# Stick-breaking attention: in each step VectorE's quarter sums and low parts first, scan and product last

## The chip, the cores and the metric

The kernel runs on one core of one Trainium2 chip. The metric is the device time of one execution in microseconds (us), taken as the median of several runs.

## The reference, cut to what matters

Two transformer blocks run one after the other on a sequence of 1024 rows of width 1024, in float32. The first has pooling, a sliding-window attention, a feed-forward part and a gate; the second has two kinds of attention, an output projection and a gated feed-forward part with a short convolution. The change lies in the second block's stick-breaking attention (8 heads of 64 features):

```python
for blk in range(s // SB_BLOCK):                 # 8 blocks of 128 queries
    logits = einsum("bqhd,bkhd->bhqk", q[:, q_start:k_end], k[:, :k_end]) * scale
    strict = (q_start + arange(SB_BLOCK))[:, None] > arange(k_end)[None, :]
    log_beta = log_sigmoid(logits)
    log_keep = where(strict, log_sigmoid(-logits), 0.0)
    log_tail = cumsum(log_keep, reverse=True) - log_keep
    weights = where(strict, exp(log_beta + log_tail), 0.0)
    outs.append(einsum("bhqk,bkhd->bqhd", weights, v[:, :k_end]))
```

The weight of a key is sigmoid(logit) times the product of sigmoid(-logit) over all later keys that the query may see. The kernel makes this product with a running multiplication, a scan, instead of logarithms.

## The kernel before, in words

Float32 products are made in three passes of a faster format: each operand is split in a high part (rounded by ScalarE, `..._hi`) and a low part (source minus high part, made by VectorE, `..._lo`). Every result that becomes an operand again so passes ScalarE first and then VectorE.

The stage around the change handles 4 pairs of heads. For each pair, `BSTEPS` lists 24 blocks: for each query tile `qt` of 128 rows, for each of the two heads, a first chunk of up to four key tiles and, for `qt` above 3, a second chunk with the rest. A block has 1 to 4 tiles of 128 keys. All 96 blocks (`NS`) are numbered by z; `stick_step(z)` gives pair, head, query tile, chunk and tiles. Each engine runs a loop over steps s written out by hand, in which it handles different blocks, so that the stages of one block follow each other:

- ScalarE, step s: `turned_hi(s-3)` (L2049) rounds the turned weights from PSUM to `wt` (L2054), then `signs(s)` (L2038) makes `keep` = sigmoid(-x) (L2044) and `stick` = sigmoid(x) (L2047) from the logits; then high parts of projections and weights, and for a finished quarter `quarter_low` (L2060) and `quarter_move` (L2065). `signs(s)` waits for VectorE's product of block s-2.
- GpSimd, step s: `cut(s)` (L864) zeroes `stick` on and above the diagonal for blocks with a diagonal; then the sums of finished quarters (L875) and of their squares (L884, L890, L893).
- VectorE, step s: `tails(s-1)` (L2669) makes the scan over `keep` into `tail` (L2675) and the product `stick` times `tail` (L2682), which waits for `stick` or the cut; `turned_lo3(s-3)` (L2684) makes the low half of the turned weights in `wt` from PSUM (L2687), and waits for ScalarE's rounded half of block s-3, made in the same step s; `quarter_add(d)` (L2690) adds the two halves of a quarter of the output (L2692) five steps after the quarter's last block, 32 times in all. Behind these stand `job_lo` (low parts of the projection for the next pair, L2301, L2305, L2308), `beside3` (in step 16 the inverse roots for another normalisation, L2698 to L2704; near the end the output weights L2718 and the turned rows L2712) and `stick_weight_lo` (low part of a weight unit, L2288).
- TensorE, step s: `turn3(s-2)` (L1547) transposes the weights of block s-2; it waits for VectorE's product of s-2 and for the low part of s-4. `outputs3(s-4)` (L1563) multiplies turned weights and values. In odd steps `scores3(s+1)` (L1513) makes the logits of the next two blocks and waits for `stick` of block s. Then `jobs3` (L918 to L920) makes a part of the next pair's projection (steps 0 to 71), and in steps 78 to 93 `first_half_row` makes the first half of the output projection.

The order in each engine's loop is the only thing that sets the order of its work. VectorE's loop is L2740 to L2756:

```python
for s in range(NS + 7):
    if 1 <= s <= NS:
        tails(s - 1)
    if 3 <= s < NS + 3:
        turned_lo3(s - 3)
    d = quarter_ended(s - 5)
    if d is not None:
        quarter_add(d)
```

Of the kernel before, what the change touches and what calls it, by code (L numbers as in the profile page):

```python
# [72 lines left out]
class Chain:  # L73
# [13 lines left out]
    def link(self, ins):  # L87
        ins.then_inc(self.sem, 1)
        self.n += 1
        if self.at is None:  # L90
            self.eng.wait_ge(self.sem, self.base + self.n)
        else:
            self.eng.wait_ge(self.sem, self.at * self.per + (self.base + self.n))


def build(nc, x, p, w_in, w_pool, pool_scale, attn_sinks, w_out, ln1_g, ln1_b, w_ff1, w_ff2,
# [8 lines left out]
    with ctx:  # L105
# [318 lines left out]
        NS = 4 * NB  # L424

        def stick_step(z):

            hh, qt, c = BSTEPS[z % NB]
            nt = qt - 3 if c else min(qt + 1, 4)
            return z // NB, hh, qt, c, nt, 0 if c else qt + 1 - nt  # L430
# [6 lines left out]
        def diagonals(z):  # L437

            return sum(stick_step(i)[3] == 0 for i in range(z + 1))
# [13 lines left out]
        def quarter_ended(z):  # L453

            return quarter_of(z) if 0 <= z < NS and stick_step(z)[2:4] in ((1, 0), (3, 0), (5, 1), (7, 1)) else None
# [7 lines left out]
        def quarter_bank(hh):  # L463

            return pt[:, hh, :].rearrange("p (a b n) -> p a b n", b=2, n=P)
# [39 lines left out]
        def stick_ends(s):  # L505

            return [job[:4] for job in stick_jobs(s) if job[4] == KT - 1]
# [81 lines left out]
        def next_unit(q, e):  # L589

            u = {1: 3 * q + 2, 3: 3 * q + 3, 6: 3 * q + 4}[e]
            return u if u < 24 else None
# [9 lines left out]
        def _(sp):  # L602
# [19 lines left out]
            for c, (u, slot, _, _) in enumerate(SEG["in"]["rows"]):  # L622
                room("in", None, c)
                if c < 2:
                    for r in range(4 * c, 4 * c + 4):
                        sp.dma_start(acc[:, r, :], x[r * P:(r + 1) * P, :]).then_inc(x_in[c], 16)
                if c < 6:
                    col = c * P if c < 4 else 1024 + (c - 4) * P
                    sp.dma_start(raw_k(slot, 0, 8), w_in_t[:, :, col:col + P]).then_inc(raw_in[slot], 16)
                else:  # L630
                    for hh in range(2):
                        col = 512 + 64 * (c - 6) + 256 * hh
                        sp.dma_start(raw_k(slot, 0, 8)[:, :, 64 * hh:64 * hh + 64],
                                     w_in_t[:, :, col:col + 64]).then_inc(raw_in[slot], 16)
# [60 lines left out]
            with sp.Fori(0, SEG["gate"]["n"]) as i:  # L695
                for c, (u, slot, _, _) in enumerate(SEG["gate"]["rows"]):
                    room("gate", i, c)
                    sp.dma_start(raw_k(slot, 0, 8), gate_t[:, :, ds((i * 2 + c) * P, P)]).then_inc(raw_in[slot], 16)
                    sp.dma_start(raw_k(slot, 8, 10), ple_t[:, :, ds((i * 2 + c) * P, P)]).then_inc(raw_in[slot], 16)
# [1512 lines left out]
        def _(dve):  # L2212
# [71 lines left out]
            def stick_weight_lo(u):  # L2284
                if u is not None:
                    hi, lo, src, _, n = stick_unit(u)
                    dve.wait_ge(split_hi, n)
                    dve.tensor_tensor(lo, src, hi.bitcast(F32), ALU.subtract).then_inc(w_ready, 1)  # L2288

            def job_lo(i, n, kv, ends, q, q_slot=0, one=False):  # L2290

                for e, kind, half in ends:
                    if kind == "V":
                        continue
                    dve.wait_ge(jb_hi, i * (2 * NJ2) + (n + e + 1))
                    bank = 0 if one else BANK3[e] if q is not None and q != "alone" and q >= 5 else half
                    src = pd[:, q_slot if kind == "Q" else 0, bank * HB:(bank + 1) * HB]
                    cols = slice(half * HB, (half + 1) * HB)
                    if kind == "Q":
                        hi, lo = kv["q"]  # L2300
                        dve.scalar_tensor_tensor(out=lo[:, cols], in0=src, scalar=QSCALE, in1=hi[:, cols].bitcast(F32),  # L2301
                                                 op0=ALU.mult, op1=ALU.subtract).then_inc(jb_lo, 1)
                    elif kind == "K":
                        hi, lo = kv["k"]
                        dve.tensor_tensor(lo[:, cols], src, hi[:, cols].bitcast(F32), ALU.subtract).then_inc(jb_lo, 1)  # L2305
                    else:
                        v = kv["v"][:, 4 * half:4 * half + 4, :, :]
                        dve.tensor_tensor(v[:, :, :, 64:P], src.rearrange("p (r h c) -> p r h c", h=2, c=64),  # L2308
                                          v[:, :, :, 0:64].bitcast(F32), ALU.subtract).then_inc(jb_lo, 1)
# [359 lines left out]
            def tails(z):  # L2669
                pair, hh, qt, c, nt, kt0 = stick_step(z)  # L2670
                f, n, c1 = hh, nt * P, S - (qt + 1 - kt0 - nt) * P
                kept = keep[:, z % 2, 0:n][:, ::-1]
                dve.wait_ge(b_keep, z + 1)
                bound = kept if c else passed[:, HB - n:HB][:, ::-1]
                link(dve.tensor_tensor_scan(tail[:, f % 2, c1 - n:c1][:, ::-1], kept, bound,  # L2675
                                            tail[:, f % 2, c1:c1 + 1], ALU.mult, ALU.min if c else ALU.max))
                w = stick[:, z % 3, 0:n]
                if c:
                    dve.wait_ge(b_stick, z + 1)
                else:  # L2680
                    dve.wait_ge(b_cut, diagonals(z))
                dve.tensor_tensor(w, w, tail[:, f % 2, c1 - n + 1:c1 + 1], ALU.mult).then_inc(b_w, 1)  # L2682

            def turned_lo3(z):  # L2684
                n = stick_step(z)[4] * P
                dve.wait_ge(b_wh, z + 1)
                dve.tensor_tensor(wt[:, z % 2, 1, 0:n], pt[:, 2 + z % 2, 0:n], wt[:, z % 2, 0, 0:n].bitcast(F32),  # L2687
                                  ALU.subtract).then_inc(b_ws, 1)

            def quarter_add(d):  # L2690
                dve.wait_ge(q_low, d + 1)
                dve.tensor_tensor(quarter[d % 2][:, :, :], quarter_bank(d % 2)[:, :, 0, :], quarter[d % 2][:, :, :],  # L2692
                                  ALU.add).then_inc(q_added, 1)
# [27 lines left out]
            def beside3(s):  # L2721
                if s == 16:
                    dve.wait_ge(oa_sq, 8)
                    inverse_roots(rsq_a[:, :], ssq[:, 0:8], HB)
                    dve.sem_inc(oa_roots, 1)
                if 72 <= s < 76:
                    mix_weight_lo(s - 72)
                if 75 <= s < 79:
                    for b in range(2 * (s - 75), 2 * (s - 74)):
                        mixed_lo(b, pd[:, 0, b % 2 * HB:(b % 2 + 1) * HB])  # L2730
                if s == 80:
                    dve.sem_inc(m_free, 8)
                if 94 <= s < 98:
                    mix_weight_lo(s - 90)
                if 95 <= s < 97:
                    for b in range(2 * s - 182, 2 * s - 180):
                        mixed_lo(b)

            link(dve.memset(tail[:, :, S:S + 1], 1.0))
            for s in range(NS + 7):  # L2740
                if 1 <= s <= NS:
                    tails(s - 1)
                if 3 <= s < NS + 3:
                    turned_lo3(s - 3)
                d = quarter_ended(s - 5)
                if d is not None:
                    quarter_add(d)
                if 1 <= s <= 3 * NB + 2:
                    for q, e, kind, half in stick_ends(s - 1) + stick_ends(s - 2):
                        if (kind == "T") == ((q, e, kind, half) in stick_ends(s - 1)):  # L2750
                            job_lo(0, 4 * NJ1 + NJ2 * q, att2[q % 2], [(e, kind, half)], q)
                beside3(s)
                if 1 <= s <= 3 * NB + 2:
                    for q, e, kind, half in stick_ends(s - 2):
                        if kind != "T" and half:
                            stick_weight_lo(next_unit(q, e))  # L2756
# [168 lines left out]
```

## Time and profile before

| | us |
|---|---|
| median of 3 runs | 2544.61 |
| lowest and highest run | 2543.91, 2546.9 |
| the profiled execution | 2542.35 |
| its span, first to last instruction | 2540.4 |
| TensorE busy in the span | 2449.6 |
| VectorE busy | 1499.6 |
| ScalarE busy | 848.3 |
| GpSimd busy | 278.6 |

The mean granted clock of TensorE is 0.990 of full speed. Busy times of TensorE count overlapping matmuls by their covered time. The stick-breaking loop runs from about 1458 to 1751 us of the span. PE is TensorE, PEld its weight load, DVE VectorE, ACT ScalarE, POOL GpSimd.

### The profile page before, as it was taken

What the parts mean: (1) busy time and instruction counts of PE and PEld (TensorE: products, weight loads), DVE (VectorE), ACT (ScalarE), POOL (GpSimd) and SP (SyncE); (2) the same over time, 40 slices, a digit from 0 to 9 for tenths busy, and PEclk for the clock granted to TensorE, in tenths of its full rate; (3) what the DMA queues carried; (4) which work ended last, traced back from release to release, by engine and by line L of the source; (5) the groups of instructions that cost most, each with busy time, mean ns of one, the idle gap of its engine ahead of it and who ended that gap; (6) DMA issues with size and microseconds to landing.
All of it is one profiled execution on the core that took longest, in us unless ns stands there. A gap on an engine that the chain in (4) does not pass through costs nothing.

```text
span 2540.4 us, 31692 instructions
## 1 busy us (share of the span) xinstructions
PE 2449.6 (96%) x11970; PEld 2027.8 (80%) x11970; DVE 1499.6 (59%) x2087; ACT 848.3 (33%) x1517; POOL 278.6 (11%) x212
## 2 busy tenths in 40 slices
PE   8999999999999999998999999988999999999998
PEld 6787878888888888787788877767788888888886
DVE  5685564444434447546444499977675555656466
ACT  2374421011101102536444476665612020212122
POOL 4333100000000000001222233331000000000000
PEclk9999999999999999998999999998999999999999
DMA  4553032232322223113111001021111120202011
GB/s 124 32 43 121 21 100 79 75 104 82 91 88 91 87 76 113 38 38 121 34 41 31 26 18 34 17 100 42 42 60 57 34 66 22 70 23 74 25 59 75
DMA packets 201574, 156.99 MB, mean 62 GB/s; under 512 B 56185, under 2 KB 176513, under 8 KB 201473
## 3 DMA queue, kind: packets, MB, share of 16 engines
q1 hardware_dynamic: 183344, 124.94, 17.0%
q10 hardware_dynamic: 18128, 30.71, 4.8%
q8 instruction: 63, 1.03, 0.2%
q14 instruction: 39, 0.31, 0.0%
HBM read 147.23 MB, written 11.56 MB: 63 GB/s over the span
## 4 chain that ended last, share of the span: by engine, by line
PE 86%; DVE 7%; ACT 3%; issue 2%; DMA 1%; SPq 0%; POOL 0%; ACTq 0%; DVEq 0%; POOLq 0%
PE pd L918 25%; PE pd L920 25%; PE pd L919 25%; PE pt L1471 1%; PE pd L1513 1%; PE pd L1440 1%; DVE tail L2675 1%; PE pt L1563 1%; PE pt L1489 1%; PE pt L1547 1%; PE pt L938 1%; PE pt L918 1%; PE pt L919 1%; PE pt L920 1%; DVE wt L2687 0%
## 5 line engine op out<-in xcount | busy, mean ns | idle before, releaser
L918 PE MATMUL pd<-actT_hi,st_hi 128*128 128x512 f32 x1872 | 745.6, 398 | 7.0 <-DVE st_lo L2458 3.5
L920 PE MATMUL pd<-actT_hi,st_lo 128*128 128x512 f32 x1872 | 732.2, 391 | 0.0
L919 PE MATMUL pd<-actT_lo,st_hi 128*128 128x512 f32 x1872 | 731.5, 391 | 0.0
L918 PEld LDWEIGHTS pd<-actT_hi,st_hi 128*128 128x128 f32 x1872 | 353.0, 189 | 82.8 <-issue 8.7
L920 PEld LDWEIGHTS pd<-actT_hi,st_lo 128*128 128x128 f32 x1872 | 352.7, 188 | 75.8
L919 PEld LDWEIGHTS pd<-actT_lo,st_hi 128*128 128x128 f32 x1872 | 353.4, 189 | 66.1
L918 PE MATMUL pd<-mv_hi,hid_hi 128*128 128x512 f32 x864 | 337.0, 390 | 3.8 <-DVE acc L2763 1.5
L919 PE MATMUL pd<-mv_lo,hid_hi 128*128 128x512 f32 x864 | 336.2, 389 | 0.0
L920 PE MATMUL pd<-mv_hi,hid_lo 128*128 128x512 f32 x864 | 336.2, 389 | 0.0
L1863 ACT ACTIVATE mv_hi<-raw 128x1024 fp32r<-128x1024 f32 x54 | 55.9, 1056 | 602.3 <-PE pd L920 477.9
L1708 ACT ACTIVATE evac<-pd 128x1024 f32<-128x1024 f32 x76 | 77.9, 1024 | 451.2 <-PE pd L920 451.2
L2421 DVE TENSOR_TENSOR acc<-acc,pd 128x1024 f32<-128x1024 f32 x72 | 87.9, 1221 | 184.7 <-PE pd L920 184.7
L814 POOL TENSOR_TENSOR st_hi<-raw,ones 128x1024 fp32r<-128x1024 f32 x27 | 65.8, 2439 | 1192.7 <-DMA raw<-in_w_in 906.1
L918 PEld LDWEIGHTS pd<-mv_hi,hid_hi 128*128 128x128 f32 x864 | 162.2, 188 | 39.3 <-DVE acc L2763 2.9
L920 PEld LDWEIGHTS pd<-mv_hi,hid_lo 128*128 128x128 f32 x864 | 162.2, 188 | 33.8
L919 PEld LDWEIGHTS pd<-mv_lo,hid_hi 128*128 128x128 f32 x864 | 162.2, 188 | 33.4
L2458 DVE TENSOR_TENSOR st_lo<-raw,st_hi 128x1024 fp32r<-128x1024 f32 (+1 forms) x83 | 103.6, 1250 | 118.9 <-ACT st_hi L1863 113.4
L2762 DVE TENSOR_TENSOR gated<-pd,row_b 128x1024 f32<-128x1024 f32 x48 | 58.8, 1225 | 103.5 <-PE pd L920 103.2
L1863 ACT ACTIVATE st_hi<-raw 128x1024 fp32r<-128x1024 f32 (+1 forms) x83 | 89.0, 1075 | 55.7 <-DMA raw<-in_w_ff 20.3
L2845 DVE TENSOR_SCALAR cv<-evac,cw,cb 128x1024 f32<-128x1024 f32 x44 | 35.7, 811 | 119.3 <-ACT evac L1708 118.1
L2458 DVE TENSOR_TENSOR mv_lo<-raw,mv_hi 128x1024 fp32r<-128x1024 f32 x54 | 65.0, 1223 | 59.5 <-ACT mv_hi L1863 58.3
L2620 DVE CUSTOM_DVE_ANT_0 prob<-pd,bias 128x640 f32<-128x640 f32 (+4 forms) x64 | 42.0, 658 | 82.2 <-PE pt L1471 80.5
(354 smaller groups left out, 3577.6 us busy)
## 6 DMA issues: line engine op xcount, KB each, us to landing
raw<-in_w_ff SPq DMA_DIRECT2D x64, 512.0 KB, 4.0
ada_raw<-in_w_ada ACTq DMA_DIRECT2D x64, 384.0 KB, 3.2
raw<-in_w_up SPq DMA_DIRECT2D x44, 512.0 KB, 3.8
raw<-in_w_in SPq DMA_DIRECT2D x30, 512.0 KB, 3.8
raw<-in_w_down SPq DMA_DIRECT2D x22, 512.0 KB, 3.3
acc<-in_x SPq DMA_DIRECT2D x16, 512.0 KB, 6.6
raw<-in_w_out SPq DMA_DIRECT2D x12, 512.0 KB, 3.2
raw<-in_w_ple_gate SPq DMA_DIRECT2D x8, 512.0 KB, 3.7
```

The costliest lines, as they stand in the source:

```text
L814: pool.tensor_tensor(hi.rearrange("p (k n) -> p k n", n=P), src.rearrange("p (k n) -> p k n", n=P), ones[:, :].unsqueeze(1).to_broadcast([ ...
L918: pe.matmul(out_ap, a_hi, b_hi, start=start, stop=False, skip_group_check=check)
L919: pe.matmul(out_ap, a_hi, b_lo, start=False, stop=False, skip_group_check=check)
L920: return pe.matmul(out_ap, a_lo, b_hi, start=False, stop=stop, skip_group_check=check)
L938: last = pe.transpose(pt[:, job % 4, r * P:(r + 1) * P], src[:, half * 4 + r, kt * P:(kt + 1) * P], ident[:, :])
L1708: act.activation(buf[:, t % 2, :], pd[:, t % 2, :], func, **kw).then_inc(t_free, 1)
L1863: act.activation(hi, src, ACT.Copy).then_inc(split_hi, 1)
L2421: return dve.tensor_tensor(acc[:, r, :], acc[:, r, :], pdr(r), ALU.add)
L2458: dve.tensor_tensor(lo, src, hi.bitcast(F32), ALU.subtract).then_inc(w_ready, 1)
L2620: dve.tensor_tensor_reduce(out=prob2[:, z % 2, 0:n], in0=x, in1=bias2[pair % 2][:, hh, NA - n:NA], scale=-1.0, scalar=3e38, op0=ALU.add, o ...
L2762: link(dve.tensor_tensor(gt[:, :], pdr(r), row_gate[:, :], ALU.mult))
L2845: link(dve.tensor_scalar(y, u, cw[:, 2, ds(f, 1)], cb[:, ds(f, 1)], ALU.mult, ALU.add))
```

## The change

In VectorE's loop the three calls that open a step are put in the opposite order: the quarter sum first, then the low part of the turned weights, and scan and product last of the three. What follows them in the step keeps its place. Each call issues the same instructions with the same waits as before, and no other engine's program is touched.

```diff
             for s in range(NS + 7):
-                if 1 <= s <= NS:
-                    tails(s - 1)
-                if 3 <= s < NS + 3:
-                    turned_lo3(s - 3)
                 d = quarter_ended(s - 5)
                 if d is not None:
                     quarter_add(d)
+                if 3 <= s < NS + 3:
+                    turned_lo3(s - 3)
+                if 1 <= s <= NS:
+                    tails(s - 1)
                 if 1 <= s <= 3 * NB + 2:
                     for q, e, kind, half in stick_ends(s - 1) + stick_ends(s - 2):
```

## Rows read from the trace of the kernel before

**Rows 1.** The page: the span, and VectorE's busy time and share.
```profile
span 2540.4 us, 31692 instructions
...
PE 2449.6 (96%) x11970; PEld 2027.8 (80%) x11970; DVE 1499.6 (59%) x2087; ACT 848.3 (33%) x1517; POOL 278.6 (11%) x212
```

**Rows 2.** Stretches: length, busy us (instructions) of PE PEld DVE ACT POOL, clock, DMA.
```profile
1690.00:1737.00 47.00, 46.67 (x254) 37.37 (x252) 27.76 (x39) 26.86 (x54) 12.31 (x14) 1.00 0.00 0
...
sum 300.00, PE 276.37 PEld 220.37 DVE 260.04 ACT 199.71 POOL 100.79; mean PE 27.64 PEld 22.04 DVE 26.00 ACT 19.97 POOL 10.08
```

**Rows 3.** VectorE's groups by shape, 1457 to 1757: busy, mean ns | idle before.
```profile
L2675 DVE TENSOR_TENSOR_SCAN tail<-keep,tail,passed 128x512 f32<-128x512 f32 x40 | 55.0, 1375 | 0.5 <-ACT keep L2044 0.2
L2682 DVE TENSOR_TENSOR stick<-stick,tail 128x512 f32<-128x512 f32 x48 | 42.3, 880 | 3.9 <-POOL stick L864 2.7
L2687 DVE TENSOR_TENSOR wt<-pt,wt 128x512 fp32r<-128x512 f32 x48 | 32.9, 686 | 15.2 <-ACT wt L2054 15.0
...
L2692 DVE TENSOR_TENSOR quarter_b<-pt,quarter_b 128x256 f32<-128x256 f32 x16 | 6.6, 415 | 1.0 <-ACT quarter_b L2060 1.0
```

**Rows 4.** Waits, 1457 to 1757: who for whom, total us, times, longest.
```profile
DVE wt L2687 <- ACT wt L2054: 20.2, 20, 2.6
...
PE pt L1547 <- DVE wt L2687: 10.9, 7, 4.2
```

**Rows 5.** Timeline around block 9: start us, us, engine, line.
```profile
1479.95 0.69 DVE L2687 TENSOR_TENSOR wt<-pt,wt 128x512 fp32r<-128x512 f32 x1 [0.88 <-ACT wt L2054]
1480.56 0.68 DVE L2301 SCALAR_TENSOR_TENSOR q_lo2b<-pd,q_hi2b 128x512 fp32r<-128x512 f32 x1
1481.16 1.24 DVE L2288 TENSOR_TENSOR st_lo<-raw,st_hi 128x1024 fp32r<-128x1024 f32 x1
1481.41 1.59 POOL L875 TENSOR_TENSOR rows<-rows,quarter_b 64x256 f32<-64x256 f32 x1
1482.32 1.76 DVE L2675 TENSOR_TENSOR_SCAN tail<-keep,tail,passed 128x512 f32<-128x512 f32 x1
1482.93 0.60 PE L1547 MATMUL pt<-ident,stick 128*128 128x128 f32 x4
1484.12 0.92 DVE L2682 TENSOR_TENSOR stick<-stick,tail 128x512 f32<-128x512 f32 x1
1484.96 0.68 DVE L2687 TENSOR_TENSOR wt<-pt,wt 128x512 fp32r<-128x512 f32 x1
1485.78 0.63 PE L1547 MATMUL pt<-ident,stick 128*128 128x128 f32 x4 [0.40 <-DVE wt L2687]
```

**Rows 6.** Timeline around block 41.
```profile
1566.97 0.42 DVE L2687 TENSOR_TENSOR wt<-pt,wt 128x256 fp32r<-128x256 f32 x1
...
1569.04 1.31 DVE L2675 TENSOR_TENSOR_SCAN tail<-keep,tail,passed 128x512 f32<-128x512 f32 x1
1570.38 0.69 DVE L2682 TENSOR_TENSOR stick<-stick,tail 128x512 f32<-128x512 f32 x1
1570.99 0.42 DVE L2687 TENSOR_TENSOR wt<-pt,wt 128x256 fp32r<-128x256 f32 x1
1572.26 0.60 PE L1547 MATMUL pt<-ident,stick 128*128 128x128 f32 x4
```

**Rows 7.** Timeline around block 16, then around block 37.
```profile
1503.48 0.42 DVE L2687 TENSOR_TENSOR wt<-pt,wt 128x256 fp32r<-128x256 f32 x1
...
1504.14 0.60 PE L1547 MATMUL pt<-ident,stick 128*128 128x128 f32 x4
...
1561.05 0.28 DVE L2687 TENSOR_TENSOR wt<-pt,wt 128x128 fp32r<-128x128 f32 x1
1561.89 0.60 PE L1547 MATMUL pt<-ident,stick 128*128 128x128 f32 x4
```

**Rows 8.** Timeline around block 88, where TensorE has extra work.
```profile
1712.34 0.42 DVE L2687 TENSOR_TENSOR wt<-pt,wt 128x256 fp32r<-128x256 f32 x1 [1.33 <-ACT wt L2054]
...
1718.80 0.60 PE L1547 MATMUL pt<-ident,stick 128*128 128x128 f32 x4
```

## The prediction

> **What bounds the kernel now.** I read the page first: the span is 2540.4 us and VectorE is busy for 59% of it [rows 1]. The change touches one loop only, the stick-breaking stage, so next I cut the span into stretches. The stage fills the stretch from 1457 to 1757. There TensorE is busy for 276.4 of 300 us and VectorE for 260.0 [rows 2]. VectorE is close behind TensorE here, unlike in the rest of the kernel. So about 24 us of TensorE's idle time is at stake, and any time by which VectorE comes later than TensorE can bear.
>
> I call the 96 rounds of work blocks, 0 to 95. In its step s TensorE turns block s-2 and multiplies block s-4 with the values; VectorE makes the scan and the product of block s-1 and the low part of block s-3. The turn of block z waits for two things: the product of z and the low part of z-2. Both are made by VectorE in one step, z+1. **Which of them comes first inside the step is therefore nothing to TensorE**; it waits for the later one. The waits of the stage say so: TensorE waits 10.9 us in 7 places for a low part, the last piece of VectorE's step, and VectorE itself waits 20.2 us in 20 places for ScalarE's rounded half, which its low part needs [rows 4]. It is this second wait that the change moves.
>
> **The change part by part.** Nothing is added or removed. No DMA and no other queue is moved; each step issues the same VectorE instructions in another order.
>
> The prices: for a block of four tiles the scan averages 1.38 us, the product 0.88, the low part 0.69, and a quarter sum takes 0.42 [rows 3].
>
> 1. The low part goes ahead of scan and product. The scan and product of block s-1 need ScalarE's outputs of step s-1, the low part of s-3 needs ScalarE's rounded half of the same step s, and that needs TensorE's turn of s-3 and product of s-5. Before, VectorE had scan and product to do while that half was made; now it stands still until it lands and has scan and product behind it. In the 20 places where VectorE waited already, the start of the low part is set from outside and stays; scan and product, done before it until now, come after it. VectorE is then behind by one scan and product, 1569.04 to 1571.07, 2.03 us for four tiles [rows 6].
>
> What is late next: the product of the step, so TensorE's turn, and behind it, in VectorE's queue, the low parts of the projections and weights. Where TensorE has slack this costs nothing. In the timeline VectorE ends its step ahead of most turns, at block 37 by 0.56 (the low part ends at 1561.33, the turn starts at 1561.89) [rows 7] and at most others by more. Late in the stage the slack is largest: the low part of block 86 starts at 1712.34 after a wait and the turn of block 88 at 1718.80 [rows 8]. With 0.42 for the low part and 2.03 for scan and product, VectorE would end at 1714.8, still 4.0 us ahead. The 16 steps in which TensorE also makes the first half of the output product (about 60 us) cost nothing; if TensorE's 12 extra passes were gone there, the cover would be too.
>
> It costs where an external wait is followed by a long step. **Block 9** is the clearest [rows 5]. The low part of block 6 starts at 1479.95, after a wait of 0.88. Then come a projection's low part (1480.56), a weight's (1481.16), scan and product of block 9 (1482.32 and 1484.12, ending 1485.04) and the low part of 7, which ends at 1485.64; the turn of block 9 starts at 1485.78, 0.14 later. There is no slack. In the new order the same start gives: low part 0.61 (start to start), scan and product of block 8 2.03, the two low parts 1.76, low part of 7 0.60, scan and product of block 9 2.03 clean or 2.72 as now beside GpSimd. That ends at 1486.98 to 1487.67, against 1485.64: late by 1.34 to 2.03. I take 1.5, nearer the low end, because GpSimd's work (from 1481.41) would fall mostly beside the weight's low part and only a little beside a scan. The turn of block 8 (1482.93) is met: its product would end at 1482.6. The place recurs in each of the three pairs of heads that project the next pair (blocks 9, 33, 57): 3 x 1.5 = **4.5 us**.
>
> **Block 41** [rows 6]: here the low part of 38 starts at 1566.97. New order: 0.34, then 2.03, the two low parts 1.76, the next low part 0.34, then 2.03: ends at 1573.47, where now the step's end is 1570.99 + 0.42 = 1571.41. Late by 2.06; the turn stands at 1572.26, 0.85 later, of which 0.14 is the hand-over, so 0.71 is slack: **1.35 us**. The third pair has no weight to split at that place (the stream ends), so it has no such loss.
>
> **Blocks 16 and 17**: now the low part of 14 ends at 1503.90 and the turn of 16 starts at 1504.14 [rows 7], again no slack. The inverse roots lie before it. The full 2.03 of displaced work would show here, of which 1.5 was already paid at block 9: **0.6 us**. Two near misses, block 37 and its like in the third pair, 61, I put at 0.1 each, **0.2**.
>
> 2. The quarter sum goes to the front. It was behind scan, product and low part; now it delays the product by 0.42 in 32 of the steps [rows 3]. In none of the places above does such a step come before the late turn; elsewhere slack hides it. If the slack there were gone it would be 32 x 0.42 = 13.4 us, the upper bound. On the other side ScalarE, which moves the quarter on, gets it up to 2 us earlier. ScalarE isn't what TensorE waits for at the late turns, so I take 0.
>
> 3. The final steps (94, 95), where TensorE waits up to 4.2 us [rows 4], are set by the output weights' parts, which stand behind the moved pieces in both orders: 0.
>
> Sum: 4.5 + 1.35 + 0.6 + 0.2 = **+6.65 us**. The stage's lost time isn't won back later: what follows is serial. The profiled execution took 2542.35 us (span 2540.4 and 1.95 around it); with the sum, 2549.0. It lies 2.3 us under the median of the runs, 2544.61. The forecast is for the median: 2544.61 + 6.65 = **2551.3 us**. A measurement of this kernel can tell about 0.2%, 5.1 us, from no change.
>
> **A rule against the trace.** A product of four tiles takes 0.69 when alone, yet 0.92 where GpSimd works beside it, and a scan then 1.76 instead of 1.31 [rows 5, 6]. The low part, with one input in PSUM, keeps 0.68 to 0.69. The Trainium skill (SBUF, "Who interferes with whom") says that a VectorE instruction with two SBUF inputs contends with a GpSimd instruction that reads SBUF, one with at most one SBUF input doesn't. The trace agrees. Taken to its end, the rule would have the change gain, since the immune low part now fills the moment in which GpSimd runs: that is the second rival.
>
> **The rivals.**
> *All hidden.* Seven stalls in 96 steps is few; if ScalarE's halves come earlier, helped by the earlier quarter sums, each loss shrinks to under 0.7. For it: most turns have slack. Against it: at blocks 9, 33, 57 the slack is zero and the start is fixed by ScalarE, busy without a gap. Time: 0 to +4, so about 2546.6. Chance 0.27.
> *Faster, by the collisions.* Mechanism: GpSimd's cut releases the product and GpSimd's next sum together, so they collide. The 48 large products average 0.19 above 0.69, 9 us, and the 40 large scans about 0.07 above 1.31, 3 us [rows 3, 6]. If the new order keeps them apart and VectorE's ready halves cost no wait, the stalls on VectorE (10.9 us) fall by up to 5: 2540. It decides only if at block 9 more than the displaced 2.03 comes back; the two collisions there give 0.69. Chance 0.07.
> *Lag spreads to ScalarE.* ScalarE's step s waits for the product of s-2 before it makes the next keep and stick values, and TensorE's scores of every second step wait for these. If the later product holds this ring, each of the 36 pairs of steps before the sheltered stretch loses about 0.3: +11, and 2562 with the sum's 6.65. For it: VectorE waits for ScalarE in 20 places already. Against it: scores stand behind turn and outputs, which wait for the same product. Chance 0.13.
> *My forecast*, the named places and nearly no others, +4 to +10: chance 0.53.
>
> **How the numbers follow.** Faster by over 0.2%: 0.05 (the collision case, less its mild part). Slower by over 0.2%: 0.13 plus the part of the forecast above 5.1 us, 0.45 of its 0.53, in all 0.58. Within: 0.37. The range runs from 2544.5 (nearly all hidden) to 2559 (most of the spreading case); outside remain the gains and the worst of the spreading.
>
> **What would show it.** In the new profile the wait of the low part for ScalarE should grow from 20.2 us to 50 or more while VectorE's busy time stays within a few us of 260. TensorE's wait should change its name, from the low part to the product, and be some 7 us larger, at blocks 9, 17, 33, 41, 57. The stretch of 47 us before 1737 should keep its length. It is wrong if block 9's turn isn't later, or if the growth is spread evenly over all pairs of steps, or if VectorE's busy time falls by over 8 us.

## The result and the profile after

| | before | after |
|---|---|---|
| median, us (20 runs of each on the same chip) | 2545.54 | 2554.26 |
| lowest and highest run | 2542.40, 2550.01 | 2548.20, 2559.77 |
| the profiled execution | 2542.35 | 2555.22 |
| its span | 2540.4 | 2553.3 |
| mean granted clock | 0.990 | 0.987 |

The ratio of after to before is 1.0033 [1.0027, 1.0039]: the change costs 8.7 us. The forecast was slower, 2551.3 in a range of 2544.5 to 2559.0.

First the page of after, answering [rows 1]:

```profile
span 2553.3 us, 31692 instructions
...
PE 2458.4 (96%) x11970; PEld 2031.1 (80%) x11970; DVE 1492.7 (58%) x2087; ACT 850.6 (33%) x1517; POOL 280.7 (11%) x212
```

VectorE is busy for 6.9 us less in a span 12.9 us longer. So the change saves busy time and still loses time: what it costs must be waits. In the after trace the first turn of the stage starts at 1464.73, against 1462.55 before, with no changed instruction ahead of it. These 2.18 us are a difference between two executions and are left out from here on: every "later by" below counts from the turn of block 0 in the same trace.

Next the waits of the stage, 1457 to 1772 us of after (who waits for whom, total us, times, longest), answering [rows 4]:

```profile
DVE wt L2687 <- ACT wt L2054: 40.6, 35, 2.5
ACT keep L2044 <- DVE stick L2682: 30.4, 31, 2.4
...
PE pt L1547 <- DVE stick L2682: 17.6, 13, 4.1
```

The low part waits for ScalarE's rounded half in 35 places instead of 20 and for twice as long, 40.6 us instead of 20.2. TensorE's wait has changed its name, from the low part to the product, and grown from 10.9 to 17.6 us. A third wait has grown most: ScalarE waits 30.4 us for the product, where the same view of before has 4.9 us in 6 places.

VectorE's groups by shape over 1457 to 1770 (busy us, mean ns | idle before), answering [rows 3]:

```profile
L2675 DVE TENSOR_TENSOR_SCAN tail<-keep,tail,passed 128x512 f32<-128x512 f32 x40 | 52.7, 1317 | 0.0
L2682 DVE TENSOR_TENSOR stick<-stick,tail 128x512 f32<-128x512 f32 x48 | 36.4, 757 | 1.7
L2687 DVE TENSOR_TENSOR wt<-pt,wt 128x512 fp32r<-128x512 f32 x48 | 32.9, 686 | 13.6 <-ACT wt L2054 13.2
```

The products have become faster by 5.9 us and the scans by 2.3; the low parts took 32.9 us before and take 32.9 now. This is where VectorE's lower busy time comes from.

Then stretches of after (length; busy us and instructions of PE, PEld, DVE, ACT, POOL; granted clock; DMA share; GB/s), answering [rows 2]:

```profile
1457.00:1770.00 313.00, 284.66 (x1584) 225.16 (x1585) 252.09 (x392) 201.76 (x443) 102.64 (x124) 0.95 0.13 43
1702.00:1749.00 47.00, 47.00 (x256) 37.80 (x255) 27.00 (x40) 26.63 (x56) 11.67 (x14) 1.00 0.00 1
1558.00:1562.00 4.00, 4.00 (x15) 2.69 (x15) 2.67 (x7) 2.34 (x5) 1.01 (x2) 0.58 0.00 0
```

TensorE is again busy for all of the sheltered 47 us. The last of the three rows is new in kind: TensorE is busy for all 4 us, but at a granted clock of 0.58 (1.00 is full speed).

To find where the time goes I took the start of TensorE's turn (L1547) of each block in both traces and subtracted. The lateness grows in a few jumps:

| turn of block | later by, us | what was added since the row above |
|---|---|---|
| 8 | 0.00 | |
| 9 | 1.08 | 1.08 at block 9 |
| 32 | 1.78 | 0.38 at 13, 0.12 at 14, 0.34 at 16, 0.31 at 17 and 18, -0.50 at 20, 0.05 after |
| 33 | 3.21 | 1.43 |
| 34 | 4.72 | 1.51, at the lower clock |
| 38 | 5.56 | 0.73 at 37, 0.11 at 38 |
| 42 | 6.85 | 1.10 at 41, 0.20 at 42 |
| 56 | 6.84 | nothing |
| 57 | 8.18 | 1.34 |
| 58 | 9.70 | 1.52, at the lower clock |
| 62 | 10.54 | 0.73 at 61, 0.11 at 62 |
| 78 to 91 | 10.5 | nothing (between 71 and 77 it moves from 9.7 to 11.4 and back) |
| 95 | 10.41 | |

Block 9 shows the mechanism. The timeline of after (start us, us, engine, line, out<-in, idle before), answering [rows 5]:

```profile
1482.12 0.69 DVE L2687 TENSOR_TENSOR wt<-pt,wt 128x512 fp32r<-128x512 f32 x1 [1.83 <-ACT wt L2054]
1482.73 1.27 DVE L2675 TENSOR_TENSOR_SCAN tail<-keep,tail,passed 128x512 f32<-128x512 f32 x1
1484.04 0.69 DVE L2682 TENSOR_TENSOR stick<-stick,tail 128x512 f32<-128x512 f32 x1
1484.65 0.68 DVE L2301 SCALAR_TENSOR_TENSOR q_lo2b<-pd,q_hi2b 128x512 fp32r<-128x512 f32 x1
1485.25 1.21 DVE L2288 TENSOR_TENSOR st_lo<-raw,st_hi 128x1024 fp32r<-128x1024 f32 x1
1486.38 0.68 DVE L2687 TENSOR_TENSOR wt<-pt,wt 128x512 fp32r<-128x512 f32 x1
1486.99 1.27 DVE L2675 TENSOR_TENSOR_SCAN tail<-keep,tail,passed 128x512 f32<-128x512 f32 x1
1488.29 0.69 DVE L2682 TENSOR_TENSOR stick<-stick,tail 128x512 f32<-128x512 f32 x1
1489.04 0.66 PE L1547 MATMUL pt<-ident,stick 128*128 128x128 f32 x4 [1.48 <-DVE stick L2682]
```

The low part of block 6 starts at 1482.12, which less the 2.18 is 1479.94, and before it was 1479.95: ScalarE's half sets this start in both kernels. Before, VectorE waited 0.88 us for it, now 1.83, because it comes to it with nothing done. What it had already done by then before, one scan and one product, stands behind the wait now (1482.73 to 1484.65, 1.92 us). All that follows in the queue moves, and TensorE stands idle for 1.48 us ahead of the turn at 1489.04.

### The profile page after: what moved, and what is told of

It reads as the page before. It is cut to its first block, busy times and chain, and to the rows that moved or that the text cites. A ratio compares the mean times of both kernels' runs of the same rounds, so it can differ in the third digit from the quotient of the medians.

```text
span 2553.3 us, 31692 instructions
## 1 busy us (share of the span) xinstructions
PE 2458.4 (96%) x11970; PEld 2031.1 (80%) x11970; DVE 1492.7 (58%) x2087; ACT 850.6 (33%) x1517; POOL 280.7 (11%) x212
## 3 DMA queue, kind: packets, MB, share of 16 engines
q8 instruction: 63, 1.03, 0.2%
## 4 chain that ended last, share of the span: by engine, by line
PE 86%; DVE 7%; ACT 3%; issue 2%; DMA 1%; SPq 0%; ACTq 0%; DVEq 0%
PE pd L918 26%; PE pd L920 25%; PE pd L919 25%; DVE tail L2675 1%; PE pt L1471 1%; PE pd L1513 1%; PE pd L1440 1%; PE pt L1563 1%; PE pt L1489 1%; PE pt L938 1%; PE pt L1547 1%; DVE stick L2682 1%; PE pt L918 1%; PE pt L920 0%; PE pt L919 0%
```

## The experiments

Each whole-kernel time is set beside runs of the kernel before on the same chip. "In the stage" is by how much the turn of block 95 is later than before, each counted from its turn of block 0.

**1. The quarter sum alone to the front** (scan and product, low part behind it in the old order).

```diff
             for s in range(NS + 7):
+                d = quarter_ended(s - 5)
+                if d is not None:
+                    quarter_add(d)
                 if 1 <= s <= NS:
                     tails(s - 1)
                 if 3 <= s < NS + 3:
                     turned_lo3(s - 3)
-                d = quarter_ended(s - 5)
-                if d is not None:
-                    quarter_add(d)
```

> Only the quarter sum goes to the front; scan and product still come before the low part. My theory (the loss comes from low parts that wait for ScalarE with scan and product behind them): no block's turn is later by more than 0.4 us, whole kernel within 1.5 us of before. Rival (the 0.42 us of each quarter sum in front of the product is a real part of the loss): up to 13 us over 32 steps, at least 3 us here.

Measured: 2547.42 against 2546.72 us, ratio 1.0007 [0.9998, 1.0016]; in the stage 1.6 us later, with jumps of 0.83 at block 33, 0.71 at 57 and -0.49 at 20, and 0.5 more between blocks 70 and 78. The waits in its stage (columns as above):

```profile
DVE quarter_a L2692 <- ACT quarter_a L2060: 13.9, 9, 3.9
...
PE pt L1547 <- DVE wt L2687: 13.0, 8, 4.2
...
DVE quarter_b L2692 <- ACT quarter_b L2060: 5.7, 6, 1.9
```

The whole is within what was expected of it; the two blocks are above their 0.4. The reason is in the first row: at the front of the step the quarter sum has a wait of its own for ScalarE, 19.6 us in 15 places for both halves, where [rows 3] show 1.0 for one of them. One such wait lies ahead of block 33, and behind it VectorE works without another wait until the late turn:

```profile
1539.97 0.42 DVE L2692 TENSOR_TENSOR quarter_a<-pt,quarter_a 128x256 f32<-128x256 f32 x1 [1.00 <-ACT quarter_a L2060]
```

By itself the early quarter sum costs a little and shows no gain.

**2. The low part alone before scan and product** (the quarter sum stays last).

```diff
             for s in range(NS + 7):
-                if 1 <= s <= NS:
-                    tails(s - 1)
                 if 3 <= s < NS + 3:
                     turned_lo3(s - 3)
+                if 1 <= s <= NS:
+                    tails(s - 1)
                 d = quarter_ended(s - 5)
```

> Only the low part goes ahead of scan and product; the quarter sum stays last. My theory: the whole loss is here, +8 to +11 us against before, at the same blocks (9, 13, 16, 33, 34, 37, 41, 57, 58, 61). Rival (both parts share it): under +6 us.

Measured: 2564.61 us (5 runs), ratio 1.0072 [1.0058, 1.0086], twice the cost of the whole change; in the stage 15.6 us later. This was a miss, and the most useful run: half of the change costs more than the change. Jumps are there at the four blocks (0.80 at 9, 1.42 at 33, 1.10 at 41, 0.55 at 57), and there are others that the whole change doesn't have: 0.57 and 0.53 at 7 and 8, 0.88 at 20, 0.59 each at 31 and 32, 1.38 at 44, 0.59 and 1.39 at 55 and 56, 1.38 at 68. Blocks 34 and 58 lose nothing (0.03 and 0.07). Its waits have two rows that were small before (1.4 and 0.7 us in the same view):

```profile
DVE wt L2687 <- ACT wt L2054: 53.1, 49, 2.4
...
ACT rows L2065 <- DVE quarter_a L2692: 6.9, 6, 1.3
...
ACT rows L2065 <- DVE quarter_b L2692: 4.2, 5, 1.2
```

In its timeline around block 7 the wait stands in front of the next one:

```profile
1475.11 0.40 ACT L2060 ACTIVATE quarter_b<-pt 128x256 f32<-128x256 f32 x1
...
1476.08 0.42 DVE L2692 TENSOR_TENSOR quarter_a<-pt,quarter_a 128x256 f32<-128x256 f32 x1
...
1476.53 0.42 ACT L2065 ACTIVATE rows<-quarter_a 64x256 f32<-64x256 f32 x1 [1.02 <-DVE quarter_a L2692]
1476.86 0.47 ACT L2054 ACTIVATE wt<-pt 128x384 fp32r<-128x384 f32 x1
...
1477.36 0.56 DVE L2687 TENSOR_TENSOR wt<-pt,wt 128x384 fp32r<-128x384 f32 x1 [0.86 <-ACT wt L2054]
```

ScalarE's move of a finished quarter (L2065) waits 1.02 us for VectorE's quarter sum, ScalarE's next rounded half stands behind the move, and VectorE's low part waits 0.86 us for that half. With the low part first, such a circle costs time; with the quarter sum at the very front, it is opened.

**3. The low part first in three steps only** (steps 9, 33 and 57, in which the low parts of blocks 6, 30 and 54 wait; everything else as before).

```diff
             for s in range(NS + 7):
+                few = s % NB == 9 and s < 3 * NB
+                if few and 3 <= s < NS + 3:
+                    turned_lo3(s - 3)
                 if 1 <= s <= NS:
                     tails(s - 1)
-                if 3 <= s < NS + 3:
+                if not few and 3 <= s < NS + 3:
                     turned_lo3(s - 3)
```

> The low part goes first in three steps of 96 only (steps 9, 33 and 57, whose low part waits for ScalarE and is followed by a projection's and a weight's low part). My theory: block 9 is later by 1.1 to 1.5 us, blocks 33 and 57 by 1.3 to 1.6 us each and the blocks after them by 1.5 us more where the granted clock falls, in all +4 to +7 us; nothing at 41. Rival (the loss is spread over the pairs of steps through ScalarE's wait for the product): under +1.5 us.

Measured: 2553.44 us, ratio 1.0023 [1.0014, 1.0032]; in the stage 8.4 us. That is above the +4 to +7 expected, and each of the three named blocks is above its range. Three exchanged steps of 96 can cost most of what the whole change costs, though not in the same amounts at each block. Jumps: 1.55 at block 9, 1.87 at 33, 1.76 at 57, nothing at 41; -0.59 at 17; and 1.50 at block 10 and 1.46 at 34, both at a lower clock, 3.0 us together. The three places where TensorE waited, in the timeline, and the stretches behind the first and the last of them:

```profile
1490.53 0.63 PE L1547 MATMUL pt<-ident,stick 128*128 128x128 f32 x4 [1.94 <-DVE wt L2687]
...
1559.42 0.63 PE L1547 MATMUL pt<-ident,stick 128*128 128x128 f32 x4 [2.28 <-DVE wt L2687]
...
1626.47 0.63 PE L1547 MATMUL pt<-ident,stick 128*128 128x128 f32 x4 [2.28 <-DVE wt L2687]
```

```profile
1490.00:1495.00 5.00, 4.47 (x19) 3.23 (x20) 4.68 (x10) 2.69 (x7) 0.71 (x1) 0.67 0.12 37
...
1626.00:1631.00 5.00, 4.53 (x28) 3.61 (x29) 4.68 (x10) 3.38 (x9) 1.05 (x1) 1.00 0.00 0
```

Idle times of 1.94 and 2.28 us were followed by a fall of the clock, another of 2.28 was not: the granted clock is 0.67 in one stretch and 1.00 in the other.

**4. After, with the weight's low part two steps later.** The long instruction L2288 (1.21 us) stood in the queue between the wait and the late product; it is given another step. The rest of the change stays.

```diff
-                if 1 <= s <= 3 * NB + 2:
-                    for q, e, kind, half in stick_ends(s - 2):
+                if 3 <= s <= 3 * NB + 4:
+                    for q, e, kind, half in stick_ends(s - 4):
                         if kind != "T" and half:
                             stick_weight_lo(next_unit(q, e))
```

> The changed kernel with the low part of each weight unit (1.22 us) two steps later, where blocks have one or two tiles or more slack. My theory: the losses at 9, 33, 41, 57 and with them the clock's falls at 34 and 58 go; 7 or more of the 10.5 us lost in the stage come back, so the kernel is within 3 us of before. Rival (the order itself costs, whatever stands behind it): at least 7 us over before.

Measured: 2549.72 us, ratio 1.0014 [1.0005, 1.0023]; in the stage 3.9 us later, so 6.5 of the 10.4 are back, a little short of what was expected. The jumps at 9 and 41 are gone, 33 has 0.35 and 57 has 0.24 left, and the clock doesn't fall at 34 or 58, which is 3.0 of the 6.5. Blocks 37 and 61 keep their losses (0.73 and 0.71), and blocks 43 and 44 lose 0.95 that after doesn't. The weight's low part gains in the old order too, by 1.8 us (experiment 7). Set against that run, the new order still costs 5.7 us here, 0.6 of them at block 9, and neither run has a fall of the clock before block 72. What is instructive is a wait that stays:

```profile
DVE wt L2687 <- ACT wt L2054: 31.6, 30, 2.5
ACT keep L2044 <- DVE stick L2682: 27.6, 33, 2.2
...
PE pt L1547 <- DVE stick L2682: 13.2, 14, 4.1
```

ScalarE still waits 27.6 us for the product, nearly all of after's 30.4, while most of the loss is gone. So ScalarE's large new wait isn't what costs the time.

**5. After, without most of the sums of squares.** From the second pair on GpSimd squares and adds one column of 256, so most of the sums of squares (for a later normalisation) are left out and GpSimd's long instructions L890 and L893 shrink.

```diff
-                    pool.tensor_tensor(sq_pair[:, :], f, f, ALU.mult).then_inc(ob_sq, 1)
+                    pool.tensor_tensor(sq_pair[:, 0:1], f[:, 0:1], f[:, 0:1], ALU.mult).then_inc(ob_sq, 1)
...
-                    pool.tensor_tensor(sq_b[n % 4][:, :], sq_b[n % 4][:, :], sq_pair[:, :], ALU.add).then_inc(ob_sq, 1)
+                    pool.tensor_tensor(sq_b[n % 4][:, 0:1], sq_b[n % 4][:, 0:1], sq_pair[:, 0:1], ALU.add).then_inc(ob_sq, 1)
```

> The changed kernel; from the second pair of heads on GpSimd squares and adds one column instead of 256 (so most of the sums of squares are left out). If GpSimd beside VectorE lengthens the product of block 33 (1.03 us) and 57 and so makes TensorE's idle time there 1.83 us instead of 1.48 as at block 9: these products take 0.69, the losses at 33 and 57 fall from 1.43 and 1.34 to 1.1 us each, those at 37 and 61 from 0.73 to 0.4 or less. If the collision is not the cause, they stay.

Measured in one run: 2551.43 us, so only its trace is used; in the stage 7.0 us. Jumps: 1.09 at 33 (1.43 in after), 0.02 at 34 (1.51), 0.00 at 37 (0.73), 1.09 at 41 (1.10), 1.00 at 57 (1.34), -0.01 at 61 (0.73). At block 70 the run is 5.3 us ahead of after, at the end 3.4. Between blocks 73 and 78 the falls of the clock lie elsewhere than in after (one here has a granted clock of 0.57 from 1681 to 1685); what makes the difference isn't settled. Block 33 in the timeline, first after with GpSimd's instruction beside it, then this run:

```profile
1554.84 1.76 POOL L893 TENSOR_TENSOR sq_b<-sq_b,sq_pair 128x256 f32<-128x256 f32 x1
...
1556.12 1.03 DVE L2682 TENSOR_TENSOR stick<-stick,tail 128x512 f32<-128x512 f32 x1
...
1557.21 0.66 PE L1547 MATMUL pt<-ident,stick 128*128 128x128 f32 x4 [1.83 <-DVE stick L2682]
```

```profile
1555.78 0.69 DVE L2682 TENSOR_TENSOR stick<-stick,tail 128x512 f32<-128x512 f32 x1
...
1556.52 0.65 PE L1547 MATMUL pt<-ident,stick 128*128 128x128 f32 x4 [1.48 <-DVE stick L2682]
```

The losses at 37 and 61 exist only by collisions of VectorE with GpSimd: in after the scan of block 37 takes 1.71 us and its product 1.05, instead of 1.27 and 0.69 clean. Of those at 33 and 57 the collisions are 0.35 us, about a quarter, of those at 9 and 41 nothing.

**6. After, with unread matmuls ahead of the three late turns.** At blocks 9, 33 and 57 TensorE first waits for the earlier of the two things that the turn needs, the low part of z-2, then makes six matmuls into the bank that the turn will overwrite, and only then waits for the product. Nothing reads what they make.

```diff
+                if z in (9, 33, 57):
+                    pe.wait_ge(b_ws, z - 1)
+                    for _ in range(6):
+                        pe.matmul(pt[:, 2 + z % 2, :], actT_hi[:, 0, 0:P], actT_hi[:, 0, 0:HB], start=True, stop=True)
```

> The changed kernel; while TensorE waits for the product of blocks 9, 33 and 57 it makes six matmuls that nobody reads, into the bank that the turn then overwrites. If the extra 1.5 us after blocks 33 and 57 is TensorE's granted clock, fallen to its lower level after the idle time: no matmul of 0.63 us follows, the blocks 34 and 58 lose nothing more, the turns of 9, 33 and 57 themselves stay late as before, whole kernel 1.5 to 3.5 us less than the changed one. If the extra comes from another wait, blocks 34 and 58 are as late as before or later.

Measured: 2553.34 us, ratio 1.0026 [1.0016, 1.0035]; in the stage 8.9 us. The turns are as late as in after (1.10 at 9, 1.44 at 33, 1.34 at 57), but blocks 34 and 58 add nothing (-0.01 and 0.04). The timeline at block 33 (lines stand 4 lower than in after), and then the same matmul of after:

```profile
1557.54 1.52 PE L1546 MATMUL pt<-actT_hi 128*128 128x512 f32 x6
1559.54 0.66 PE L1551 MATMUL pt<-ident,stick 128*128 128x128 f32 x4 [0.47 <-DVE stick L2686]
...
1561.83 0.40 PE L919 MATMUL pd<-actT_lo,st_hi 128*128 128x512 f32 x1
```

```profile
1559.55 0.79 PE L918 MATMUL pd<-actT_hi,st_hi 128*128 128x512 f32 x1
1560.14 0.63 PE L919 MATMUL pd<-actT_lo,st_hi 128*128 128x512 f32 x1
```

This parts the two costs: the lateness of the product, which the filler can't mend, and a fall of the clock behind it. Where the clock stays up, a turn as late as in after adds nothing at the next block, so the 1.5 us at 34 and 58 are the clock's. That the filler is what kept the clock up is likely but not shown: in experiments 2 and 8 the turn of block 33 came after idle times of 1.83 and 1.85 us without a filler, and the clock stayed up as well. By block 70, 3.0 us had come back; 1.5 us of that went again around blocks 74 to 78, where this run has a fall of the clock that after doesn't have (granted 0.68 in the 4 us from 1684.38). Over the whole kernel the two intervals overlap, so the gain in time is shown in this trace only.

**7. Before, with the weight's low part two steps later**: the edit of experiment 4 on the old order.

> The kernel before, with only the weight's low part two steps later. VectorE's step at blocks 9, 17, 33, 41, 57 gets 1.2 us shorter: the turn of 9, 33 and 57 comes 0.4 us earlier each, that of 17 by up to 1.6 us: 1.5 to 3.5 us less than before in the stage. If it only moves the stall to the next steps: within 0.7 us of before in the stage.

Measured: 2543.53 against 2546.47 us, ratio 0.9985 [0.9976, 0.9994]; in the stage 1.8 us earlier: -0.56 at block 9, -0.56 at 33, -0.67 at 57, -1.18 at 17, 1.14 given back at 19 and 20. It is faster than both kernels: at those blocks the same queue had no slack before the change either [rows 5].

**8. Low part first, with ScalarE's move one step later.** Experiment 2, and the move no longer asks for a sum of the same step.

```diff
-                d = quarter_ended(s - 5)
+                d = quarter_ended(s - 6)
                 if d is not None:
                     quarter_move(d)
```

> The low part first and the quarter sum last (which lost 15.6 us in the stage, 5.2 more than with the quarter sum first), with ScalarE's move of the quarter one step later, so that it no longer waits for VectorE's sum of the same step. If that wait of ScalarE, in front of its next rounded half, is what the quarter sum's early place saves: the 5.2 us come back, +9 to +12 us against before in the stage, and blocks 7, 8, 31, 32, 55, 56 lose nothing. Rival (the 0.42 us of the sum between product and the next low part): still +14 us or more.

Measured: 2553.97 us, ratio 1.0030 [1.0021, 1.0039]; in the stage 8.1 us, so 7.5 of experiment 2's 15.6 are back, more than the 5.2 expected. The jumps at 7, 31, 44, 55 and 68 are 0.00 and that at 20 is -0.50, while 9, 33, 41 and 57 keep theirs. The wait of ScalarE's move for a quarter sum is no longer in its list. One fall of the clock (1.54 at block 58) is in it. Blocks 8, 32 and 56 even have jumps of -0.3 each. So experiment 2's surplus was the circle through ScalarE's move; the places where it arose are all empty now.

**9. Before, with both later**: the weight's low part by two steps, ScalarE's move by one.

> The kernel before with the weight's low part two steps later and ScalarE's move of the quarter one step later. If ScalarE's wait for the quarter sum still holds back a rounded half in the old order, this gains on top of the 1.8 us in the stage that the weight's place alone gave: 2 to 4 us in the stage, 0.1 to 0.2% in all. If scan and product in front of the low part already cover that wait, it is the same as with the weight's place alone, within 0.4 us in the stage.

Measured: 2542.59 against 2545.31 us, ratio 0.9986 [0.9977, 0.9995]; in the stage 3.1 us earlier (-0.56 at 9, -1.55 at 17, -0.47 at 20, -0.56 at 33, -0.67 at 57, and 1.25 lost at 77, where the clock falls). Blocks 8, 32 and 56 have jumps of -0.3 each that experiment 7 doesn't have, so ScalarE's move cost time in the old order too. It too beats both kernels. Whether it beats experiment 7 the times can't tell, the intervals are the same.

## Why the prediction was right, and where it was off

**The mechanism held.** The low part waits where its start is set from outside, and the displaced scan and product come behind it [rows 4, 5]. Block 9 shows it row by row, three exchanged steps alone make the kernel 6.7 us slower (experiment 3), and with the long instruction taken out from between, the turns of 9 and 41 are no later than before (experiment 4). The displaced work is still there: against the old order with the same move (experiment 7), block 9 is 0.6 later. The named blocks were the right ones, and between them little grows.

**Term by term** (from the table of turns):

| term | forecast | measured |
|---|---|---|
| blocks 9, 33, 57 | 4.5 | 1.08 + 1.43 + 1.34 = 3.85 |
| block 41 (with 42) | 1.35 | 1.30 |
| blocks 16, 17 (all of 13 to 32) | 0.6 | 0.70 |
| blocks 37, 61 (with 38, 62) | 0.2 | 1.68 |
| quarter sum | 0 | see below |
| sheltered stretch, last steps | 0 | -0.1 |
| clock, blocks 34 and 58 | none | 3.03 |
| sum | 6.65 | 10.5 |

At block 9 I was above: 1.08 lies below even the lower bound, 1.34. The prediction took 2.03 us for a scan and product, from [rows 6], which runs to the product's end. Here the first pair took 1.92 to the start of what follows, the second 1.99 to its end, the two low parts between them 1.73 instead of 1.76, and the hand-over to TensorE was shorter by 0.08.

The term for blocks 16 and 17 met its number partly by luck: these two gave 0.45 of it, blocks 13, 14 and 18 another 0.7, and 0.50 came back at block 20, which the prediction doesn't have.

**The step that failed is the near misses, put at 0.1 each.** The prediction gives no working for it; it names a slack of 0.56 us [rows 7] and prices scan and product clean. In the new order the scan of block 37 met GpSimd's squares for longer than before (1.71 us against 1.49, the product 1.05 against 0.92), and scan and product together took 0.8 us more than clean. Experiment 5 has 0.00 at 37 and -0.01 at 61, so the collision is nearly the whole term.

**Missing altogether was the clock**, 2 x 1.5 us. The forecast made TensorE stand idle for 1.9 us at block 9, the 0.40 of [rows 5] and 1.5 more, and priced that at its length alone. At block 9 itself the clock didn't fall, at 33 and 57 it did.

**The quarter sum at 0** was right as a sum and wrong as a reading. The reason I gave against it, that ScalarE isn't what TensorE waits for, is what fell. Nor does it hold that no quarter sum stands before the late turns in a way that matters: the sum ahead of block 33, several steps earlier, delays it when nothing else takes up the wait. Alone the early quarter sum costs 1.6 us in the stage (experiment 1); given the low part in front, it brings 5.2 (15.6 without it, 10.4 with it), by keeping ScalarE's move from waiting ahead of a rounded half (experiments 2 and 8). The two edits aren't additive, and taking either alone gives a wrong picture of it.

**The whole-kernel figure** came nearer than the terms, 8.7 us against 6.65, and that is partly luck: terms too high and too low met, and the two that were missed most, the near misses and the clock, make 4.5 us. The stage of the profiled execution lost 10.4; less the two falls of the clock that is 7.4. That runs differ in how often the clock falls would explain why the medians differ by less than the traces, but I have a trace of one execution only, so this is open. For the same reason a difference of 1.5 us between the stages of two experiments can be one fall of the clock and nothing else.

**The rivals.** *All hidden* fell: the jumps are there in full. *Faster, by the collisions*: its mechanism is real. The product, which reads two SBUF inputs, went from 880 to 757 ns and the scan from 1375 to 1317 [rows 3], while the low part, with one input in PSUM, stayed at 686. That is the distinction of the Trainium skill (SBUF, "Who interferes with whom"), and the trace agrees. But VectorE's 8 us came back mostly where TensorE wasn't waiting. Of the late turns they helped at block 9 by 0.7 us (1.27 and 0.69 in place of 1.76 and 0.92) and at 33 and 57 by about 0.4 each (scans 1.27 in place of 1.75 and 1.77, products 1.03 in place of 0.92), and there the displaced 1.9 to 2.0 us outweigh them. *Lag spreads to ScalarE*: the wait that it named did appear, 30.4 us. It costs next to nothing: in experiment 4 it is still 27.6 us with 6.5 of the loss gone, and the sheltered and the quiet blocks gain no lateness.

**The signs named beforehand.** TensorE's wait did change its name and grew by 6.7 us, forecast 7. The 47-us stretch kept its length. The low part's wait came to 40.6 us, short of 50: the quarter sum in front of it, with waits of its own, took some; with the low part first of all it was 53.1 (experiment 2). VectorE's busy time fell from 260.0 to 252.1, by 7.9, more than the few us I allowed and just inside the 8 that would have told against me.

## What to carry to other kernels

When calls are reordered in a loop whose engine runs in order, look for the places where a wait has its end set by another engine, and ask what was done during the wait before: that work now comes after it, and costs up to its length where the consumer has no slack (1.08 of 1.92 us at block 9); a long instruction behind it is what used up the slack here. Look at both directions: another engine may wait in its own queue for the moved piece with your next input behind that wait, so test the parts of a reordering apart and together. A cheap remedy for such a place is to move the long instruction that nobody waits for soon to another step; with the old order that beat both kernels here, with the new one it won back most of the loss.

## What was not expected of the hardware

Inside a stretch in which TensorE is busy nearly throughout, an idle time of 1.4 to 2.3 us can be followed by a spell at the lower of its two clock levels (1.2 instead of 2.4 GHz). A matmul of 512 columns then takes 0.63 us instead of 0.40, the 4 us after the late turn have a mean granted clock of 0.58, and the next turn is 1.5 us later still, about as much as the wait itself had added. The trace of before has such a fall in this stage already, at 1657 us after an idle time of 2.28, so the forecast could have priced it. In the stretches of after the clock is back soon, here in the 4 us that follow:

```profile
1562.00:1566.00 4.00, 4.00 (x27) 3.25 (x26) 2.22 (x4) 2.55 (x6) 1.09 (x2) 0.99 0.03 6
```

It fell after idle times of 1.83 and 1.84 us (after, blocks 33 and 57), 1.94 and 2.28 (experiment 3, blocks 9 and 33), 1.85 (experiment 8, block 57), and in experiment 2 after 1.65 and even 1.37 (at 1482.55 and 1623.11, ahead of the scores). It didn't fall after 1.48 (after, block 9; experiment 5, block 33), nor after 1.83 and 1.85 at block 33 of experiments 2 and 8, nor after 2.28 at block 57 of experiment 3. Experiment 8 has both cases in one trace, the turns of blocks 33 and 57 after the same wait:

```profile
1556.89 0.66 PE L1547 MATMUL pt<-ident,stick 128*128 128x128 f32 x4 [1.85 <-DVE stick L2682]
...
1556.90:1560.90 4.00, 4.00 (x25) 3.12 (x26) 3.26 (x8) 2.75 (x7) 0.42 (x1) 1.00 0.03 8
1624.00:1628.00 4.00, 4.00 (x17) 2.93 (x18) 2.76 (x8) 1.92 (x6) 0.00 (x0) 0.57 0.00 0
```

So the length of the idle time alone doesn't decide it; what else does, these runs leave open. Nor does each fall cost 1.5 us: in experiment 2 blocks 55 to 58 lost 2.6 us together with a fall among them, and blocks 31 to 34 lost 2.6 without one. With six matmuls that nobody reads in each of three waits the clock stayed up at all three, where in after it fell at two (experiment 6). That fits a remedy, but one trace doesn't prove one.

The second surprise is how unevenly a collision with GpSimd prices the same product of 128 x 512: 0.69 us alone, and 0.92 [rows 5], 1.03 and 1.05 beside it.
